# The orders of the query/key stage, and the last two key heads scaled and transposed later in attention

## What is computed

```
q = (rms_norm(q_lat, g_qa) @ w_qb).reshape(B, S, H, QK_DIM)           # 384 -> 8 heads x (128 + 64)
kv = (rms_norm(kv_lat, g_kva) @ w_kvb).reshape(B, S, H, QK_NOPE + V_DIM)   # 256 -> 8 heads x (128 + 128)
q_nope = rms_norm(q[..., :QK_NOPE], g_q_nope)
q_pe = apply_rope(rms_norm(q[..., QK_NOPE:], g_q_rope), cos, sin)
k_nope = rms_norm(kv[..., :QK_NOPE], g_k_nope)
v = kv[..., QK_NOPE:]
k_pe = apply_rope(rms_norm(k_rope, g_k_rope)[:, :, None, :], cos, sin)  # one rotary key for all heads
...
s = einsum('bhqd,bhkd->bhqk', q_i, kh)      # causal mask, 128-query blocks
prob = softmax(s)
o = einsum('bhqk,bhkd->bhqd', prob, vh)
```

## Time and profile before

| what | value |
|---|---|
| median of 3 runs | 1094.85 us (1093.58 to 1095.67) |
| the profiled execution, its own time | 1093.05 us |
| its span in the profile | 1091.3 us |
| query/key stage, first to last projection's transposes | 213.6 to 271.9 us |
| attention | 271.9 to 333.4 us |
| TensorE clock granted in both | 1.00 |

### The profile page before, as it was taken

The page is one execution under the profiler, slowest core; times in us unless marked ns, Lnnn a source line. Parts: engine busy times, 40 slices in busy tenths (PEclk is TensorE's granted clock), DMA queues, the critical chain, the costliest instruction groups (busy, mean ns, idle before and its releaser), DMA issues.

```text
span 1091.3 us, 17848 instructions
## 1 busy us (share of the span) xinstructions
PE 1075.3 (99%) x5416; PEld 900.6 (83%) x5416; DVE 934.2 (86%) x1313; ACT 804.4 (74%) x1287; POOL 420.9 (39%) x482
## 2 busy tenths in 40 slices
PE   7999999999999999999999999999999999999998
PEld 6988888797788887888888888888888888888787
DVE  5998879587764578999999999999999999999865
ACT  7854555377553345988888888888988988888771
POOL 1100004052572003456555555555555555455400
PEclk9999999999999999999999999999999999999999
DMA  9765435023103098999999999999999999999642
GB/s 307 220 153 153 118 111 181 23 77 127 72 2 154 39 368 344 382 371 381 394 395 389 394 390 388 390 394 393 398 396 398 399 392 390 392 385 364 187 150 77
DMA packets 76504, 301.12 MB, mean 276 GB/s; under 512 B 15459, under 2 KB 20870, under 8 KB 51494
## 3 DMA queue, kind: packets, MB, share of 16 engines
q1 hardware_dynamic: 54400, 258.33, 59.4%
q0 software_dynamic: 21408, 40.04, 15.4%
q10 hardware_dynamic: 646, 2.12, 0.5%
HBM read 294.05 MB, written 42.07 MB: 308 GB/s over the span
## 4 chain that ended last, share of the span: by engine, by line
PE 93%; DVE 3%; ACT 2%; POOL 1%; issue 1%; DMA 0%; ACTq 0%; POOLq 0%; DVEq 0%
PE bank L2528 11%; PE bank L2530 11%; PE bank L2529 11%; PE bank L2155 7%; PE bank L2556 5%; PE bank L2554 5%; PE bank L2555 5%; PE bank L2493 5%; PE bank L2251 3%; PE bank L2250 3%; PE bank L2249 3%; PE bank L2193 2%; PE bank L2197 2%; PE bank L2194 2%; PE bank L2146 2%; PE bank L2407 1%
## 5 line engine op out<-in xcount | busy, mean ns | idle before, releaser
L2027 DVE TENSOR_TENSOR arena_r<-arena,win_r 128x1024 fp32r<-128x1024 f32 x252 | 291.9, 1221 | 22.0 <-ACT win_r L1301 18.7
L1301 ACT ACTIVATE win_r<-arena 128x1024 fp32r<-128x1024 f32 x252 | 246.5, 1070 | 0.5 <-DMA resid<-in_w_exp_up 0.5
L2528 PE MATMUL bank<-win_r,work_r 128*128 128x512 f32 x512 | 206.5, 403 | 0.6 <-issue 0.6
L2529 PE MATMUL bank<-win_r,x_low_r 128*128 128x512 f32 x512 | 199.5, 390 | 0.0
L2530 PE MATMUL bank<-arena_r,work_r 128*128 128x512 f32 x504 | 197.4, 392 | 0.0
L2007 DVE TENSOR_TENSOR arena_r<-arena,hT_r 128x1024 fp32r<-128x1024 f32 x128 | 150.4, 1216 | 0.5 <-ACT hT_r L1309 0.5
L872 POOL DMA_INDIRECT moe_sum<-ya,sidx x64 | 106.6, 1665 | 106.7 <-ACT ya L1337 92.9
L2530 PEld LDWEIGHTS bank<-arena_r,work_r 128*128 128x128 f32 x504 | 94.6, 188 | 21.7
L2528 PEld LDWEIGHTS bank<-win_r,work_r 128*128 128x128 f32 x512 | 96.7, 189 | 18.8 <-issue 0.7
L2529 PEld LDWEIGHTS bank<-win_r,x_low_r 128*128 128x128 f32 x512 | 96.4, 188 | 18.6
L847 POOL COPY small<-ya 128x1 f32 (+1 forms) x64 | 107.6, 1681 | 1.1 <-DMA ya<-h_rows,gidx 1.1
(11 more groups left out here) (406 smaller groups left out, 2428.8 us busy)
## 6 DMA issues: line engine op xcount, KB each, us to landing
arena<-in_w_exp_down SPq DMA_DIRECT2D x64, 1024.0 KB
arena<-in_w_exp_gate SPq DMA_DIRECT2D x63, 1024.0 KB
arena<-in_w_exp_up SPq DMA_DIRECT2D x63, 1024.0 KB
win<-in_w_in SPq DMA_DIRECT2D x10, 1024.0 KB, 5.9
resid<-in_x SPq DMA_DIRECT2D x8, 512.0 KB, 6.5
win<-in_w_in SPq DMA_DIRECT2D x2, 2048.0 KB, 9.1
win<-in_w_o SPq DMA_DIRECT2D x2, 2048.0 KB, 7.8
arena<-in_w_ple_gate SPq DMA_DIRECT2D x2, 2048.0 KB, 13.4
```

Of the source, the lines that this page charges most:

```text
L1301: act.activation(gu_hi[n % 2][:, :, cols], raw[:, :, cols], ACT.Copy).then_inc(gu_hi_r, 1)
L2027: dve.tensor_tensor(low_[:, :, cols], raw[:, :, cols], gu_hi[n % 2][:, :, cols].bitcast(F32), ALU.subtract).then_inc(gu_lo_r, 1)
L2528: pe.matmul(b_, x_hi[:, k, :], w_hi, start=(k == 0), stop=False)
L2529: pe.matmul(b_, x_lo[:, k, :], w_hi, start=False, stop=False)
```

## The change

Seven edits, all of order:
- ScalarE rounds the weights of step 1 ahead of the loop over the steps, not between the tiles of step 0.
- PE transposes the rotary key after the gating matmul g == 4 instead of ahead of it, and VectorE does `gate_a(3)` ahead of the rotary key's low part.
- PE transposes the rotated rows after the tile t == 2, not t == 1.
- VectorE makes the low parts of rotary head 0 ahead of its split of the last weight chunk, and those of head 1 behind it.
- VectorE copies one of the second pair's two transposed keys ahead of scaling the third pair and the other behind it.
- For step 7 VectorE sums three tiles (six heads' rows) in the first instruction and one tile in the second.
- In attention the last pair is scaled at VectorE's s == 6, transposed at PE's s == 9 and copied at VectorE's s == 11.

```diff
--- before.py
+++ after.py
@@ -1097,6 +1097,7 @@
                     act.activation(latT_hi[:, k, :], bank[4 + T % 2][:, :], ACT.Copy, scale=gain).then_inc(latT_hi_r, 1)
                 else:
                     act.activation(kpe_hi, bank[4 + T % 2][:, :], ACT.Copy).then_inc(latT_hi_r, 1)
+            qkv_split(1)
 
             def rope_high(h):
                 r0, T = ROPE * (h % 2), T_Q + 3 * (h // 2) + 2
@@ -1132,7 +1133,7 @@
                             act.activation(qc[s % 2][:, t, :, 0:NOPE], src[:, :, 0:NOPE], ACT.Copy)
                             act.activation(sqc[:, t, :, 0:NOPE], src[:, :, 0:NOPE], ACT.Square)
                             act.activation(V[:, t, 2 * c:2 * c + 2, :], src[:, :, NOPE:], ACT.Copy).then_inc(pj_free[n % 4], 1)
-                        if t == (0 if s == 6 else 1) and s + 1 < 8:
+                        if t == (0 if s == 6 else 1) and 1 <= s < 7:
                             qkv_split(s + 1)
                 if s == 7:
                     T = T_K + 4
@@ -1724,6 +1725,7 @@
                 if k >= 2:
                     gate_a(k - 2)
 
+            gate_a(KQ + KKV - 2)
             dve.wait_ge(latT_hi_r, KQ + KKV + 1)
             dve.tensor_tensor(kpe_lo, bank[4 + T_KPE % 2][:, :], kpe_hi.bitcast(F32), ALU.subtract).then_inc(tr_free[T_KPE % 2], 1)
 
@@ -1735,14 +1737,11 @@
                     dve.tensor_tensor(q_st[r1:r1 + ROPE, h % 2, cols], qrT[r0:r0 + ROPE, h // 2, cols],
                                       q_st[r0:r0 + ROPE, h % 2, cols].bitcast(F32), ALU.subtract).then_inc(rope_lo, 1)
 
-            for g in range(KQ + KKV - 2, G):
+            for g in range(KQ + KKV - 1, G):
                 gate_a(g)
 
-            def k_evac(c, b0):
-                if c == 1:
-                    rope_low(0)
-                    rope_low(1)
-                for h in range(1 if c == 2 else 0, 2):
+            def k_evac(c, b0, heads=(0, 1)):
+                for h in heads:
                     T = T_K + 2 * c + h
                     dve.wait_ge(tr_done, T + 1)
                     dve.tensor_copy(kT[:, 2 * c + h, :], bank[b0 + T % 2][:, :]).then_inc(tr_free[T % 2], 1)
@@ -1752,23 +1751,29 @@
                     T = T_Q + 3 * (s - 2) + 2
                     dve.wait_ge(tr_done, T + 1)
                     dve.tensor_copy(qrT[:, s - 2, :], bank[4 + T % 2][:, :]).then_inc(tr_free[T % 2], 1)
+                if s == 6:
+                    rope_low(0)
                 if s + 1 < 8:
                     qkv_split(s + 1)
+                if s == 6:
+                    rope_low(1)
                 if s < 8:
                     sq = sqc.rearrange("p t h d -> p (t h) d")
                     if s == 7:
-                        dve.wait_ge(pj_free[1], (P_Q + 4 * s) // 4 + 1)
-                        link(dve.tensor_reduce(ssq[:, 0:4], sq[:, 0:4, 0:NOPE], AX.X, ALU.add))
+                        dve.wait_ge(pj_free[2], (P_Q + 4 * s) // 4 + 1)
+                        link(dve.tensor_reduce(ssq[:, 0:6], sq[:, 0:6, 0:NOPE], AX.X, ALU.add))
                     dve.wait_ge(pj_free[3], (P_Q + 4 * s) // 4 + 1)
                     if s < 4:
                         link(dve.tensor_reduce(ssq[:, 8:16], sq[:, :, NOPE:QK], AX.X, ALU.add))
-                    r0 = 4 if s == 7 else 0
+                    r0 = 6 if s == 7 else 0
                     link(dve.tensor_reduce(ssq[:, r0:8], sq[:, r0:8, 0:NOPE], AX.X, ALU.add))
                     if s < 4:
                         mean(msq[:, 8:16], ssq[:, 8:16], ROPE, EPS)
                     mean(msq[:, 0:8], ssq[:, 0:8], NOPE, EPS).then_inc(qk_ms, 1)
-                if 5 <= s < 7:
-                    k_evac(s - 5, 4)
+                if s == 5:
+                    k_evac(0, 4)
+                if s == 6:
+                    k_evac(1, 4, (0,))
                 if s < 7:
                     dve.wait_ge(qk_rt, s + 1)
                     n = 16 if s < 4 else 8
@@ -1778,6 +1783,8 @@
                         dve.tensor_tensor(z[:, :, NOPE:QK], z[:, :, NOPE:QK], rep(msq[:, 8:16], [P, 8, ROPE], 2), ALU.mult)
                     dve.tensor_tensor(z[:, :, 0:NOPE], z[:, :, 0:NOPE], rep(msq[:, 0:8], [P, 8, NOPE], 2),
                                       ALU.mult).then_inc(qk_n, 1)
+                if s == 6:
+                    k_evac(1, 4, (1,))
 
             def last_k_norm():
                 dve.wait_ge(qk_rt, 8)
@@ -1799,10 +1806,10 @@
                 if s == NA + 1:
                     mT_low(0)
                 if s == 1:
-                    k_evac(2, 4)
-                if s == 2:
+                    k_evac(2, 4, (1,))
+                if s == 6:
                     last_k_norm()
-                if s == 7:
+                if s == 11:
                     k_evac(3, 6)
                 if s < NA:
                     W = (head_block(s)[1] + 1) * P
@@ -2284,10 +2291,11 @@
             for k in range(2, KQ + KKV):
                 mixed(k - 1)
                 lat_T(k)
-            pe.wait_ge(kp_rot, 1)
-            transposes(T_KPE, [kprot[:, t].rearrange("p h d -> p (h d)") for t in range(NT)])
             for g in range(KQ + KKV - 1, G):
                 mixed(g)
+                if g == KQ + KKV - 1:
+                    pe.wait_ge(kp_rot, 1)
+                    transposes(T_KPE, [kprot[:, t].rearrange("p h d -> p (h d)") for t in range(NT)])
 
             for i in range(2):
                 pe.wait_ge(tr_free[i], T_Q // 2)
@@ -2309,7 +2317,7 @@
                             hi, lo = latT_hi[:, k0 + k, tok(t)], latT_lo[k0 + k][:, tok(t)]
                             pairs += [(hi, w_hi[:, k, :]), (lo, w_hi[:, k, :]), (hi, w_lo[:, k, :])]
                         project(P_Q + 4 * s + t, pairs, width).then_inc(pj_done, 1)
-                        if t == 1 and 2 <= s <= 5:
+                        if t == 2 and 2 <= s <= 5:
                             pe.wait_ge(q_rot, s - 1)
                             transposes(T_Q + 3 * (s - 2) + 2,
                                        [qrot[s % 2][:, t_].rearrange("p h d -> p (h d)") for t_ in range(NT)])
@@ -2324,7 +2332,7 @@
             for i in range(4):
                 pe.wait_ge(pj_free[i], P_WO // 4)
             for s in range(NA + 2):
-                if s == 5:
+                if s == 9:
                     head_T(7, b0=6)
                 if s == 2 * H:
                     for i in range(2):
```

## The result

The changed kernel takes 1096.24 us (median of 22), the kernel before 1094.5 (22 runs beside it): ratio 1.0016, 95% interval 1.001 to 1.0022. That is 1.74 us slower, where 0.2 us faster was forecast; it lies inside the range and inside the 0.2% that counts as no change, but the sign is wrong. The profiled execution took 1096.17 us.

The account below looks back on a forecast made before the run. The prediction took the query/key stage as bound by PE and, within a microsecond, the chain ScalarE, VectorE, GpSimd. It summed -0.3 - 1.1 + 1.2 = -0.2 us from 1094.85 to 1094.65, said as 1094.6, range 1092.6 to 1096.5.

Parts of the forecast that it names:

- Head of the stage: Query/key stage before its end: early split, moved key transposes and later rotated rows together gain 0.3 us, bounds 0 and 1.5.
- End of the stage: Last steps of the query/key stage: pair's transposes no longer wait; table load and attention start 1.1 us sooner, bounds 0.7 and 1.2.
- Attention: Seventh step of attention: the moved scaling delays the maximum and PE stalls 1.2 us, bounds 0.5 and 2.4.
- the second rival: Attention's seventh step: GpSimd's L807 starts before the scaling's multiplication, which waits; price 2.4 us, total 1095.9; chance 0.17.
- Transposes and copies moved in attention: Attention's tenth and twelfth steps: transposes cost 0.87 us and the two copies 0.58, the same as before the move.
- The rivals: Stage's gain stays whole (1093.4, chance 0.22); GpSimd first at attention's seventh step (1095.9, 0.17); stage's end not sooner (1095.4, 0.08).

Follow-up runs that it names:

- tail_only: Kernel before with only the three end-of-stage edits (rotary low parts around the last split, one evacuation behind the scaling, six heads summed ahead): 1093.06 us, ratio 0.999.
- tail_again: The same kernel as tail_only, run again for its median and another profile, against the kernel before: 1093.74 us, ratio 0.9992.
- attention_only: Kernel before with only the three moves in attention (last pair's scaling, transposes and copies later): 1095.59 us, ratio 1.0011.
- late_transposes: Kernel before with the last pair transposed at attention's tenth step and copied at the twelfth, but still scaled at the third: 1093.99 us, ratio 0.9998.

## Why the prediction was wrong

- **Head of the stage, the failed step.** The sum took 0.3 us of gain for the early split, the moved key transposes and the later rotated rows, with bounds 0 and 1.5: below zero nothing. Up to step 5 the change is indeed 0.21 us ahead, though not by the key's transposes, for which 0.15 was counted. Then step 5 takes 8.66 us instead of 7.00, because the scaling gets ahead of the fourth rotation's last instruction: these edits lost about 1.45 us. Alone, the early split lost 1.87 and the later rows 1.25 and 1.08. The working followed PE and the chain behind it and said that the chain "is not shortened"; it did not ask what VectorE's earlier start, or a rotation that comes later, would run into. It had also read that weight loads already wait for the splits, so that a delay of the splits would reach PE too, and used it against a gain only. The row that shows VectorE and GpSimd holding each other up stood in the text, but it was applied to the scaling in attention alone, and not to the four scalings beside four rotations.
- **End of the stage.** Right: 1.1 us forecast, 0.91 measured in the change and 0.97 in tail_only and tail_again, from the start of step 6 to the table load; the transposes follow the projection without a wait.
- **Attention.** Right in mechanism and size: 1.2 forecast, 1.28 in the trace, 1.33 in attention_only, through the copy that stands behind the exponential. That the multiplication would come just ahead of L807 came true by 0.01 us where 0.15 was worked out: that is luck, and the second rival was close.
- **Transposes and copies moved in attention.** As forecast: the last pair's transposes and copies cost the same four steps later (late_transposes).
- **The rivals.** The slower side came from a fourth one that was not listed. With its 1.45 us the sum of the traces is 1.45 - 0.91 + 1.28 = 1.82, near the 1.74 of the medians.

The Trainium skill (SBUF — State Buffer, Who interferes with whom) says that a VectorE instruction with two SBUF inputs excludes a GpSimd instruction that reads SBUF, and that the order of issue decides who waits. The rows agree: the scaling L1784 took 1.76 us for 1.22 when GpSimd was first, GpSimd's instructions 1.18, 1.59 and 2.34 for 0.74, 0.74 and 1.28 when VectorE was.

## What to carry to other kernels

An edit that removes a wait also moves every engine behind it, and where two engines exclude each other the new position can cost more than the wait did: go along the whole chain for what each instruction will now meet, and put a loss into the bounds. Where the time sits on such an edge, profile the same code twice before reading a small difference, and try an added wait that keeps the two apart: here it gave back 1.2 us of stage. Work that was free in a start-up step is not free in a full one: look at the idle time in front of the very instruction it would precede.

## What was not expected

VectorE's two means over 8 columns, one input each, took 0.24 us in one execution and 0.81 in another. In the slow case they ended with GpSimd's L767, 0.03 us behind it, so an instruction with one SBUF input can stand behind GpSimd too. The Trainium skill (SBUF — State Buffer, Who interferes with whom) names `tensor_scalar` among the operations that can contend with GpSimd, under conditions; the rows agree. And this stall in the kernel before was of use: it kept the next scaling out of the rotation. How often the kernel before falls to the other side of that edge stays open: its single profile shows the short rotations, as do six of the eight others with the same code up to there.

It was also not expected that the first rotation's price at the start of step 3 (0.5 to 0.7 us) would hardly count: by step 5 it is made up to within 0.15 us in all four profiles that have it, and it is step 5, beside the fourth rotation, that is longer by about 1.66.
